# The chunk stage of an RWKV-7 layer: two half steps share a bank per row side, and one product with 128 stationary columns makes right side and output

## The reference

```python
def step(s, xt):                       # s: 64 x 64 state of a head
    wt, kt, vt, kkt, at = xt[:5]
    sa = einsum('bhvk,bhk->bhv', s, -kkt)
    s = s * wt[:, :, None, :] + sa[..., None] * (kkt * at)[:, :, None, :] + vt[..., None] * kt[:, :, None, :]
    return s, einsum('bhvk,bhk->bhv', s, xt[5])    # output of the token
```

## Time and profile before

| what | value |
|---|---|
| median of 3 runs | 4031.0 us (4029.63 to 4033.84) |
| the profiled execution | 4023.1 us, its span 4021.3 us |
| PE busy | 3634.7 us, 90% |
| PEld (weight loads) busy | 3022.9 us, 75% |
| DVE busy | 2190.9 us, 54% |
| ACT busy | 1844.0 us, 46% |
| mean granted TensorE clock | 0.965 |

### The profile page before, as it was taken

How to read it: one execution, slowest core, us unless ns; L and a number is a source line. 1 busy time by engine, 2 the same in 40 slices (tenths; PEclk the granted TensorE clock), 3 DMA queues, 4 the chain that set the end, 5 groups by cost and what they waited for, 6 DMA issues and landing times. The chain is left out here.

```text
span 4021.3 us, 93358 instructions
## 1 busy us (share of the span) xinstructions
PE 3634.7 (90%) x39394; PEld 3022.9 (75%) x39394; DVE 2190.9 (54%) x3518; ACT 1844.0 (46%) x2997; POOL 708.5 (18%) x901
## 2 busy tenths in 40 slices
PE   7999999999997888888787889995799999999993
PEld 6777877878786777777776767784688888888883
DVE  4553453553444666666666864456445445444545
ACT  5653543543443555555555453332344444444443
POOL 1111010010112223232221343100011111111110
PEclk9999999999998999999999999997899999999996
DMA  7566566564556443444414476654466666666667
GB/s 259 187 221 211 166 207 188 153 199 142 172 176 146 100 93 90 91 98 98 111 44 127 152 226 212 200 172 181 145 204 216 219 219 201 217 216 216 205 211 300
DMA packets 443709, 702.90 MB, mean 175 GB/s; under 512 B 182488, under 2 KB 321344, under 8 KB 425808
## 3 DMA queue, kind: packets, MB, share of 16 engines
q1 hardware_dynamic: 409504, 587.23, 47.1%
q0 software_dynamic: 33840, 110.40, 9.0%
HBM read 531.97 MB, written 165.56 MB: 173 GB/s over the span
## 5 line engine op out<-in xcount | busy, mean ns | idle before, releaser
L113 PE MATMUL fro__acc<-fro__hT_hi,fro__wh 128*128 128x512 f32 (+1 forms) x1608 | 629.4, 391 | 12.6 <-DVE fro__hT_lo L2684 8.9
L114 PE MATMUL fro__acc<-fro__hT_hi,fro__wl 128*128 128x512 f32 (+1 forms) x1608 | 614.8, 382 | 0.0
L115 PE MATMUL fro__acc<-fro__hT_lo,fro__wh 128*128 128x512 f32 (+1 forms) x1608 | 614.4, 382 | 0.0
L2014 DVE TENSOR_TENSOR fin__wl<-fin__raw,fin__wh 128x4096 fp32r<-128x4096 f32 x96 | 424.7, 4424 | 317.1 <-ACT fin__wh L1958 317.1
L2690 DVE TENSOR_TENSOR fro__wl<-prj__w,fro__wh 128x1024 fp32r<-128x1024 f32 x201 | 246.3, 1225 | 584.9 <-ACT fro__wh L2427 584.6
L1958 ACT ACTIVATE fin__wh<-fin__raw 128x4096 fp32r<-128x4096 f32 x96 | 348.4, 3629 | 191.2 <-PE exp__acc L115 190.3
L113 PE MATMUL exp__acc<-fin__wh,exp__xh 128*128 128x512 f32 x1024 | 399.9, 390 | 0.7 <-DVE exp__xl L2019 0.7
L115 PE MATMUL exp__acc<-fin__wl,exp__xh 128*128 128x512 f32 x1024 | 398.5, 389 | 0.0
L114 PE MATMUL exp__acc<-fin__wh,exp__xl 128*128 128x512 f32 x1024 | 398.5, 389 | 0.0
L113 PEld LDWEIGHTS fro__acc<-fro__hT_hi,fro__wh 128*128 128x128 f32 x1608 | 305.1, 190 | 87.3 <-issue 31.3
L115 PEld LDWEIGHTS fro__acc<-fro__hT_lo,fro__wh 128*128 128x128 f32 x1608 | 304.9, 190 | 59.2
(11 more groups left out here) (465 smaller groups left out, 7383.3 us busy)
## 6 DMA issues: line engine op xcount, KB each, us to landing
fin__raw<-in_w_x SPq DMA_DIRECT2D x96, 2048.0 KB, 8.4
prj__w<-in_w_z SPq DMA_DIRECT2D x201, 512.0 KB, 4.2
s_zT<-fro__pool SPq DMA_DIRECT2D x128, 256.0 KB, 4.6
fro__wm<-in_w_mod POOLq DMA_DIRECT2D x16, 1024.0 KB, 6.2
mix__gate<-s_zT SPq DMA_DIRECT2D x64, 256.0 KB, 4.2
rwc__ways<-s_ways SPq DMA_DIRECT2D x36, 384.0 KB, 4.5
rwc__ways<-s_ways SPq DMA_DIRECT2D x72, 192.0 KB, 4.8
rwc__both<-s_both SPq DMA_DIRECT2D x36, 384.0 KB, 4.4
```

The source lines that it names most:

```text
L113: pe.matmul(out, sh, mh, start=first, stop=False)
L114: pe.matmul(out, sl, mh, start=False, stop=False)
L115: return pe.matmul(out, sh, ml, start=False, stop=last)
L2014: ve.tensor_tensor(wl[s][:, :, :], raw[s][:, :, :], wh[s][:, :, :], ALU.subtract).then_inc(w_lo, 1)
```

## The change

Both half steps now share two banks, `QB[0]` and `QB[1]`, one per row side `x`. In each, the halves of 256 columns belong to `t = 0` and `t = 1`; the right side is on partitions 0 to 63 and the output on 64 to 127. The stationary matrix of `values` and of `from_state` gets 128 columns, and each makes right side and output in one product: 8 products instead of 16. `AR` is laid out anew for that, so that the two parts of a side stand side by side. ACT's copies to `R`, `U` and `yo` become two copies of 64 partitions each. As a first product clears the marks of a whole bank, a half step may only begin when the other is done, so `values` has new waits, and the order in the loops of PE and ACT is changed. `RB[1]`, into which `errors` and `refine` write, now lies in `QB[1]`.

```diff
-        AR = [sb(f"AR{u}", [P, 4, 2, C]) for u in range(B)]
+        AR = [sb(f"AR{u}", [P, 4, 2, 2, HC]) for u in range(B)]
...
-        PB = [room.ps(f"PB{t}", [P, 512]) for t in range(2)]
-        MB, RB = (XB, TP), (EB, PB[0])
+        QB = [room.ps(f"QB{x}", [P, 2, 256]) for x in range(2)]
+        MB, RB = (XB, TP), (EB[:, 0:256], QB[1][:, 0, :])
...
+            def rows_of(out, k, t, n):
+                for x in range(2):
+                    last = act.activation(out[side(x), :], QB[x][side(k), t, :], ACT.Copy)
+                last.then_inc(S[n], 1)
+
             def right_side(j, t):
                 act.wait_ge(S[f"rhm{t}"], at(f"rhm{t}", j))
-                cp(R[t][:, :], PB[t][:, 0:256], f"rhc{t}")
+                rows_of(R[t], 0, t, f"rhc{t}")
...
-                cp(U[t][:, :], PB[t][:, 0:256], f"uc{t}")
+                rows_of(U[t], 0, t, f"uc{t}")
...
-                cp(yo[t][:, :], PB[t][:, 256:512], f"yc{t}")
+                rows_of(yo[t], 1, t, f"yc{t}")
...
@@ ACT's loop @@
-                if exists(h - 2):
-                    right_side(h - 2, 1)
                 if inverting:
                     copies(1, h)
                 if exists(h - 2):
-                    solved(h - 2, 1)
+                    right_side(h - 2, 1)
                 if prepare:
                     scale_bk(n)
+                if exists(h - 2):
+                    solved(h - 2, 1)
                 if inverting:
                     copies(2, h)
+                if exists(h - 2):
+                    outputs(h - 2, 1)
                 if prepare:
                     scale_al(n)
+                if inverting:
+                    copies(3, h)
                 if exists(h - 1):
                     right_side(h - 1, 0)
-                if inverting:
-                    copies(3, h)
                 if prepare:
                     scale_rho(n)
-                if exists(h - 2):
-                    outputs(h - 2, 1)
                 if exists(h - 1):
                     solved(h - 1, 0)
...
@@ PE: values @@
-                if t == 0:
+                if t:
+                    pe.wait_ge(S["yc0"], at("yc0", j))
+                    if exists(j + 1):
+                        pe.wait_ge(S["gd"], at("gd", j + 1))
+                else:
                     pe.wait_ge(S["gd"], at("gd", j))
-                elif j:
-                    pe.wait_ge(S["yc1"], at("yc1", j - 1))
+                    if j:
+                        pe.wait_ge(S["yc1"], at("yc1", j - 1))
                 for q in range(4):
-                    for k in range(2):
-                        for x in range(2):
-                            r = side(x)
-                            m = mm(PB[t][r, part(k, q)], BK[u][r, 2 * q + s, 2 + k, :], v_t[u][r, head(q, x ^ s)], start=(q == 0 and k == 0), stop=False,
-                                   skip_group_check=True)
+                    for x in range(2):
+                        r = side(x)
+                        m = mm(QB[x][:, t, part(q)], BK[u][r, 2 * q + s, 2:4, :].rearrange("p k c -> p (k c)"), v_t[u][r, head(q, x ^ s)],
+                               start=q == 0, stop=False, skip_group_check=True)
@@ PE: from_state @@
                 for q in range(4):
-                    for k in range(2):
-                        for e in range(2):
-                            m = mm(PB[t][side(e ^ s), part(k, q)], AR[u][side(e), q, k, side(e ^ s)], Hb[j % 2][side(e), q, :], start=False, stop=False,
-                                   skip_group_check=True)
+                    for e in range(2):
+                        m = mm(QB[e ^ s][:, t, part(q)], AR[u][side(e), q, e ^ s, :, :].rearrange("p k c -> p (k c)"), Hb[j % 2][side(e), q, :],
+                               start=False, stop=False, skip_group_check=True)
@@ PE: solve, and outputs in the same manner with side(1) @@
-                    for r in map(side, range(2)):
-                        m = mm(PB[t][r, part(0, q)], Gr[j % 2][r, n // GH, n % GH, :], R[t][r, part(0, q)], start=False, stop=True, skip_group_check=True)
+                    for x, r in enumerate(map(side, range(2))):
+                        m = mm(QB[x][side(0), t, part(q)], Gr[j % 2][r, n // GH, n % GH, :], R[t][r, part(q)], start=False, stop=True, skip_group_check=True)
@@ PE's loop @@
-                if exists(h - 2):
-                    values(h - 2, 1)
-                    from_state(h - 2, 1)
                 if inverting:
                     couple(0, h)
...
                 if inverting:
                     double(0, h)
                 if exists(h - 2):
+                    values(h - 2, 1)
+                    from_state(h - 2, 1)
+                if inverting:
+                    couple(1, h)
+                if exists(h - 2):
                     solve(h - 2, 1)
                 if inverting:
-                    couple(1, h)
-                if exists(p):
-                    values(p, 0)
+                    double(1, h)
+                if exists(h - 2):
+                    outputs(h - 2, 1)
                 if inverting:
-                    double(1, h)
+                    couple(2, h)
                 if exists(h - 2) and exists(h):
                     state(h - 2, 1)
                 if inverting:
-                    couple(2, h)
+                    double(2, h)
                 if exists(p):
+                    values(p, 0)
                     from_state(p, 0)
-                if inverting:
-                    double(2, h)
-                if exists(h - 2):
-                    outputs(h - 2, 1)
                 if inverting:
                     couple(3, h)
```

More of the change, by code:

```diff
@@ L337, in alpha @@
                     gp.wait_ge(S["rhm1"], at("rhm1", j - B))
-                gp.tensor_tensor(AR[j % B][:, :, 0, :], ld[j % LB]["kkn"][:, :, :], e_al[:, :, :], ALU.mult).then_inc(S["al"], 1)
+                gp.tensor_tensor(AR[j % B][:, :, :, 0, :], halves(ld[j % LB]["kkn"]), halves(e_al), ALU.mult).then_inc(S["al"], 1)
             def rho(j):
                 gp.wait_ge(S["erho"], at("erho", j))
-                gp.tensor_tensor(AR[j % B][:, :, 1, :], ld[j % LB]["rS"][:, :, :], e_rho[:, :, :], ALU.mult).then_inc(S["rho"], 1)
+                gp.tensor_tensor(AR[j % B][:, :, :, 1, :], halves(ld[j % LB]["rS"]), halves(e_rho), ALU.mult).then_inc(S["rho"], 1)
             def residue(j, g):
@@ L570, in errors @@
                 ve.wait_ge(S["imt"], at("imt", j, g + 1))
-                tt(Er[:, g, :, :], h4(RB[g]), ImT[:, g, :, :], ALU.add).then_inc(S["ed"], 1)
+                tt(Er[:, g, :, :], rb4(RB[g]), ImT[:, g, :, :], ALU.add).then_inc(S["ed"], 1)
             def rounded_error(j, g):
@@ L580, in refine @@
                     ve.wait_ge(S["tti"], at("tti", j))
-                tt(Gr[j % 2][:, g, :, :], h4(RB[g]), (TTm if r == 1 else TT32)[:, g, :, :], ALU.add).then_inc(S["gd"], 1)
+                tt(Gr[j % 2][:, g, :, :], rb4(RB[g]), (TTm if r == 1 else TT32)[:, g, :, :], ALU.add).then_inc(S["gd"], 1)
             def state(j, t):
@@ L661, in pairs @@
                                 m = mm(MB[z][s][side(e ^ s), c:c + 128].rearrange("p (a c) -> p a c", a=2), src[side(e), q, side(e ^ s)],
-                                       AR[u][side(e), q, :, side(e ^ s)], start=True, stop=True)
+                                       AR[u][side(e), q, e ^ s, :, :], start=True, stop=True)
                 m.then_inc(S["m1"], 1)
@@ L730, in errors @@
                     for z in map(side, range(2)):
-                        m = mm(h4(RB[g])[z, h, :], BK[j % B][z, GH * g + h, 0, :], T32[z, g, h, :], start=True, stop=True)
+                        m = mm(rb4(RB[g])[z, h, :], BK[j % B][z, GH * g + h, 0, :], T32[z, g, h, :], start=True, stop=True)
                 m.then_inc(S["em"], 1)
@@ L742, in refine @@
                     for z in map(side, range(2)):
-                        m = mm(h4(RB[g])[z, h, :], left[z, g, h, :], right[z, g, h, :], start=True, stop=True)
+                        m = mm(rb4(RB[g])[z, h, :], left[z, g, h, :], right[z, g, h, :], start=True, stop=True)
                 m.then_inc(S["gm"], 1)
@@ L794, in state @@
                             r = side(e ^ s)
-                            m = mm(EB[side(e), part(0, q)], key[r, head(q, e)], val[r, part(0, q) if val is U[t] else head(q, e)],
+                            m = mm(EB[side(e), part(q)], key[r, head(q, e)], val[r, part(q) if val is U[t] else head(q, e)],
                                    start=(val is not U[t] and q == 0), stop=val is U[t], skip_group_check=True)
@@ L802, in outputs @@
                 for q in range(4):
-                    for r in map(side, range(2)):
-                        m = mm(PB[t][r, part(1, q)], BK[u][r, 2 * q + s, 1, :], U[t][r, part(0, q)], start=False, stop=True, skip_group_check=True)
+                    for x, r in enumerate(map(side, range(2))):
```

(1 more changed line is left out.)

3 lines of the change are left out of this document (2 added, 1 removed).

## The result

The changed kernel takes 4148.4 us (median of four runs, 4142.7 to 4152.1) against 4032.2 us for the kernel before in the same comparison: a ratio of 1.0288 (95% interval 1.0270 to 1.0305), 116 us slower. 4047 had been forecast, with 4095 as the upper end. Throughout, runs of the same state are compared; one run of the kernel before, at 9900 us with a granted clock of 0.62, is left out.

The account below looks back on a forecast made before the run. PE's products with their instruction supply, and the inverse's chain between PE and DVE or ACT, were taken as bounds; +2.86 - 2.9 + 0.5 = +0.46 us a slab, +16 us over 34 bodies, gave 4047 us, range 3990 to 4095.

Parts of the forecast that it names:

- standstills gone: Chunk stage, PE: idle time without a semaphore, read as late instruction blocks, 2.9 us a slab, taken off the sum.
- at the full granted clock: Chunk stage: PE read as busy 323.5 of 385 us, first among engines, with the clock at its full granted level.
- As width eats what the count saves: `values` and `from_state`: half the matmuls at 55.5 ns instead of 31, so 0.4 us less a slab at most.
- The rival of loads that don't pair: Wide weight loads don't run side by side: 3.3 us more a slab, 4159 us; chance 0.05.
- I price a copy of 64 partitions the same: ACT's six added copies a slab: 0.28 us each, as for full copies, 1.7 us more; bounds none and 0.38.
- the walk: New order followed from `bonus` to `couple(4)`: new waits of PE add 2.86 us to a slab.
- hidden except where PE waits for it: ACT's 1.7 us of added copies a slab is hidden, on an engine busy 12.7 of 23.8 us, unless PE waits.
- Of 2.9 us I keep 0.5: PE's standstills left in the chunk stage after the change: 0.5 us a slab, bounds 0 and 1.5.
- The rival that the standstills stay: Standstills don't come from the count of instructions, so the waits add 97 us: 4128 us; chance 0.07.
- The faster rival: Instruction supply decides, so fewer instructions shorten a slab, to 21.6 us at best: 3955 to 4022 us; chance 0.28.
- Over the 34 loop bodies: The sum of +0.46 us a slab, applied to the loop bodies with both half steps: +16 us.
- the likeliest case: The forecast itself, waits nearly balanced by fewer standstills: 4039 to 4085 us; chance 0.43.

Follow-up runs that it names:

- filled: Changed kernel plus a product nobody reads ahead of both `solve`, of `outputs` and of `couple(4)`, where PE would wait; 4128.0 us, 1.0252 of before.
- order_and_split: Kernel before with the new loop order and copies of 64 partitions, keeping its narrow products and old banks; 4121.4 us, 1.0234 of before.
- narrow_two: Changed kernel with 16 narrow products in `values` and `from_state`, column half outermost, so two quarters are used at a time; 4110.5 us, 1.0187 of before.
- tuned_tail: Changed kernel reordered for the shared banks, with second half of `state`, `refine(1)` and DVE's `state` moved too; wide products kept; 4042.9 us, 1.0080 of before.
- narrow_banks: Changed kernel with `values` and `from_state` made again of 16 narrow products each, on four quarters of the array; 4087.4 us, 1.0154 of before.
- tuned_narrow: Changed kernel with an order made for the shared banks and narrow products on four quarters; 4071.1 us, 1.0098 of before.
- tuned: Changed kernel, wide products and split copies kept, with PE, ACT and DVE reordered to put other work into the waits; 4052.4 us, 1.0052 of before.

## Why the prediction was wrong

The direction was right, and so were the waits and the standstills that were to trade places. The direction had some luck in it: +2.86 and -2.4 left +0.46 us, and the four errors below (waits, standstills left, clock, end of the stage) all happened to go up. The size was wrong, since the granted clock was in no term and made half of the miss. In the terms of the sum, per slab:

| term | predicted | measured |
|---|---|---|
| waits of the new order, to the end of `couple(4)` (a body at full clock) | +2.86 | +3.61 |
| standstills gone | -2.9 | -2.9 |
| standstills left (stretch) | +0.5 | +1.03 |
| sum | +0.46 | +1.74 (bodies at full clock: 25.52 - 23.72 = +1.80) |
| clock | no term | +1.5 (mean bodies: 3.30 in all, less 1.80) |

3.30 x 34 = 112 us; with the 18 us behind the last `bonus`, which had no term either, that is nearly the stage's whole growth of 131 us between the two profiled executions (873 to 1004 us).

1. **The failed step: "at the full granted clock".** It was read off the stretch of before and kept for the changed kernel. The mean body is 1.77 us longer than one at full clock (27.29 - 25.52), where before it was 0.27; the line through the bodies gives the same (5.7 x 0.32 = 1.8). filled speaks for more work in the idle spots raising the clock and lowering the time. The prediction had counted four idle spots a body and a PE at 1.00, and never asked whether one holds with the other. All the same, the idle spots alone don't do it: order_and_split has larger waits than the kernel after and is at half clock for 2.9 us a body, not 5.7; narrow_two, in after's own order, for 2.3. Nor does the wide product alone: tuned_tail has it, with short waits, and is at half clock for 1.1 us. The two together lower the clock; by what in the wide product stays open.

2. **"As width eats what the count saves".** The step was right in itself: the wide matmuls start 56 ns apart ((1.11 - 0.27) / 15), the weight loads take 188 ns as in the earlier trace rows, and a call takes 0.91 and 1.02 us. The rival of loads that don't pair had the wrong mechanism, though by luck its 4159 is the closest number of all. But the comparison was with the narrow products of the old banks. Beside narrow products on the new ones the wide form costs 61 us, in part by the clock and in part by the calls themselves: from the start of `values` to the bulk of `couple(1)` are 1.93 us in the kernel after (1720.97 to 1722.90) and 0.96 us in narrow_banks (1695.88 to 1696.84). The Trainium skill says both halves of it: "TensorE: Matmul & The Clock Gate", part 3 on packing small matmuls, has tiles of different row and column positions run side by side, and "TensorEngine Tiling (Array Packing)", Gotcha 1, has different row tiles write to different banks. The trace agrees with the first: 15 ns a matmul on four quarters, 56 for one that does the work of two. That the bank per row side is what allows it is not shown: four quarters over one bank weren't run, and the kernel before has both row halves write one bank at 30 ns a matmul, no slower than two quarters over two banks. The layout of the change offers it, and the wide product gives it up.

3. **"I price a copy of 64 partitions the same"** (0.28 us). Measured 0.39 to 0.40: a pair holds ACT for 0.77 to 0.79 us instead of 0.56. It is one of several parts of the 0.75 us by which the walk fell short. By the starts in the body above, 0.29 arose in the two pairs of `values` and `from_state` (1.93 us to the next `couple` where 1.78 had been taken), some 0.37 where a pair of copies stands ahead of PE (0.12 at `outputs`, 0.25 at `couple(4)`), and the rest between them. For the copy the bound of 0.38 was the better value. And "hidden except where PE waits for it" needed a price: in the old order the split alone costs 39 us.

4. **"Of 2.9 us I keep 0.5"**: 1.03 were left, inside the bounds of 0 and 1.5. Fewer instructions and more waits do go with fewer of them (46.8 to 14.6 us in the stretch), and they come back where as many matmuls as before meet a denser PE (31.7 in narrow_banks, 50.3 in tuned_narrow); with as many matmuls but large waits, in order_and_split, they are 15.7. The rival that the standstills stay (4128) was wrong: they fell by two thirds.

5. **The faster rival** wanted less than 2.2 us of the waits to come true; 3.6 did. tuned shows what it had right: with the waits removed, 616 matmuls and loads run a full-clock body in 23.68 us. It isn't less than the 23.72 of before, as the waits for `yo` (13.9 us in the stretch, 0.9 us a slab) and others took the place of the standstills.

6. **"Over the 34 loop bodies".** What comes behind the last `bonus` was left out. It takes 42 to 51 us in all nine kernels with the shared banks, the tuned ones included, and 32 to 38 in the six with the old banks, so it goes with the shared banks. The clock there is 0.70 instead of 1.00; how much of the 18 us is the clock and how much the waits stays open.

Two slips of the prediction's arithmetic changed nothing: 1.46 us a slab over 34 bodies gives 4081 as the upper end of the likeliest case, not 4085, and 155 blocks in 28.9 slabs are 5.4 a slab and some 254 instructions each, where 5.3 and 258 were used on. And none of its three signs of being wrong came true (`U` is held by `e_bk`, the standstills fell, the wide matmuls start 56 ns apart): they watched the steps that held.

The parts add up loosely: order and split copies 94 us, the rest (sharing the banks and the wide product) some 22 to 26. Narrow products on the old banks (1.0234) are slower than narrow_two on the new ones (1.0187) with the same order and copies; the gain, about 19 us, is of the size of what the meeting column halves save in the calls (an estimate from 30 and 24 ns a matmul: 0.17 us a call, four a slab, 23 us), less the longer end of the stage (48 us against 38). On these banks the wide product lost 45 to 61. It costs more than the order (33) or the split copies (39) alone, though less than the two together, and it was hidden because what it was compared with had become better too.

## What to carry to other kernels

When a layout puts each row half's results into a bank of its own, try narrow products that walk over all four quarters of the array before a wide one: here 32 narrow ones take 0.49 us and 16 wide ones 0.91. It pays only while PE has waits to spare: in the orders without them the supply of instructions took it back (1.0098 against 1.0052). A new order must be priced with its idle spots twice, as waits and as granted clock: with several spots of 0.4 to 1.0 us in a body of 25 us and the wide product, the stretch ran at 0.92 instead of 1.00, and filling four of them gave back 14 to 20 us. Look at the end of a pipelined loop too, where nothing fills the waits: here it was 18 us of the loss. And an engine that is half idle is not free: look for the wait behind each of its queues before giving it six more copies.

## What the runs showed of the hardware

- ACT: copies of 256 columns over 64 partitions follow each other 0.39 us apart, over 128 partitions 0.28, and 128 columns over 128 partitions 0.17. Two copies of half the partitions hold the engine for 0.78 us, nearly three times one full copy in a row.
- PE, float32, 64 rows, 64 moving columns, start to start: 15 ns on four quarters, 29 to 34 ns on two quarters (the diagonal in one bank, or one column half over two banks), 56 ns with 128 stationary columns on two row halves.
- A us at the lower clock level costs 0.32 us in this stage (line through 33 bodies of the kernel after; 0.31 to 0.42 in seven kernels with the standstills as a second term).
- Standstills of PE without a semaphore end 1.1 to 1.6 us after a block of the instruction queue (59 of 59 in the stretch of the kernel before). They depend on the traffic of the loads: 2.9 us a slab with the DMA share at 0.42, 1.5 us with it at 0.12.
